# Adding the diagonal mask of turned attention scores on VectorE, in the banks, instead of with a product on TensorE

## The reference, cut to what matters

```python
s = einsum('bcgrd,bkgd->bcgrk', qc, keys) * 64 ** -0.5      # scores of a query with every key
p = masked_softmax(s, key_position <= query_position)       # exp(s - row maximum), other entries are zero
o = einsum('bcgrk,bkgd->bcgrd', p, values)
```

## Time and profile before

| what | value |
|---|---|
| time, median of 3 runs (range) | 895.42 us (895.35 to 897.48) |
| time of the profiled execution | 894.6 us |
| its span in the trace | 892.6 us |
| TensorE busy | 867.4 us (97% of the span) |
| VectorE busy | 611.5 us (69%) |
| ScalarE busy | 495.1 us (55%) |
| GpSimd busy | 174.0 us (19%) |
| nsa attention in the trace | from 145.3 us to about 211.8 us |
| moba attention in the trace | from 295.8 us to about 322 us |

### The profile page before, as it was taken

How to read it: one execution, slowest core, us unless ns; L and a number is a source line. 1 busy time by engine, 2 the same in 40 slices (tenths; PEclk the granted TensorE clock), 3 DMA queues, 4 the chain that set the end, 5 groups by cost and what they waited for, 6 DMA issues and landing times.

```text
span 892.6 us, 14774 instructions
## 1 busy us (share of the span) xinstructions
PE 867.4 (97%) x5801; PEld 789.1 (88%) x5801; DVE 611.5 (69%) x974; ACT 495.1 (55%) x782; POOL 174.0 (19%) x189
## 2 busy tenths in 40 slices
PE   3999999999999999999999999999999999999998
PEld 3789898998688989999998888799998999999886
DVE  5884788978868787666665556596668666666552
ACT  3634767564747656544444447687765644444431
POOL 1026355563054710000000004280000000000000
PEclk9999999999999999999999999999999999999999
DMA  9956655456472565666667555553345566665650
GB/s 362 364 204 212 213 189 190 124 177 208 138 258 88 189 209 160 198 189 189 189 189 216 160 155 186 165 165 95 115 124 175 178 194 188 186 188 186 205 176 24
DMA packets 45844, 163.38 MB, mean 183 GB/s; under 512 B 5200, under 2 KB 5584, under 8 KB 45776
## 3 DMA queue, kind: packets, MB, share of 16 engines
q1 hardware_dynamic: 45776, 162.44, 57.3%
HBM read 161.37 MB, written 1.05 MB: 182 GB/s over the span
## 4 chain that ended last, share of the span: by engine, by line
PE 87%; DVE 5%; ACT 4%; issue 2%; DMA 1%; SPq 0%; POOL 0%; DVEq 0%; ACTq 0%
PE bank L518 36%; PE bank L506 33%; PE bank L533 3%; PE bank L865 2%; PE bank L703 2%; PE bank L680 2%; DVE ada_acc L1748 1%; DMA x<-in_x 1%; PE bank L705 1%; PE bank L656 1%; PE bank L613 1%; PE bank L684 1%; ACT w_hi L1104 1%; DVE w_lo L1663 1%; PE bank L707 1%
## 5 line engine op out<-in xcount | busy, mean ns | idle before, releaser
L1104 ACT ACTIVATE w_hi<-w_raw 128x1024 fp32r<-128x1024 f32 (+2 forms) x249 | 259.5, 1049 | 224.7 <-PE bank L518 121.3
L1663 DVE TENSOR_TENSOR w_lo<-w_raw,w_hi 128x1024 fp32r<-128x1024 f32 (+2 forms) x249 | 301.4, 1221 | 76.4 <-ACT w_hi L1104 75.7
L518 PE MATMUL bank<-h_hi,w_hi 128*128 128x256 f32 x904 | 254.4, 281 | 0.2 <-ACT tok_k L1108 0.2
L518 PE MATMUL bank<-h_lo,w_hi 128*128 128x256 f32 x904 | 251.6, 278 | 0.0
L518 PE MATMUL bank<-h_hi,w_lo 128*128 128x256 f32 x904 | 251.5, 278 | 0.0
L518 PEld LDWEIGHTS bank<-h_lo,w_hi 128*128 128x128 f32 x904 | 171.3, 189 | 0.5 <-issue 0.2
L518 PEld LDWEIGHTS bank<-h_hi,w_hi 128*128 128x128 f32 x904 | 169.8, 188 | 1.3 <-issue 0.9
L518 PEld LDWEIGHTS bank<-h_hi,w_lo 128*128 128x128 f32 x904 | 169.7, 188 | 0.0
L506 PE MATMUL bank<-w_hi,h_hi 128*128 128x512 f32 (+1 forms) x240 | 95.7, 399 | 0.8 <-issue 0.5
L2533 POOL TENSOR_TENSOR ada_acc<-ada_acc,w_raw 128x512 f32<-128x512 f32 x56 | 82.3, 1471 | 68.4 <-ACT w_raw L1108 63.3
L506 PE MATMUL bank<-w_lo,h_hi 128*128 128x512 f32 (+1 forms) x240 | 93.1, 388 | 0.0
(11 more groups left out here) (321 smaller groups left out, 1402.8 us busy)
## 6 DMA issues: line engine op xcount, KB each, us to landing
w_raw<-in_weights SPq DMA_DIRECT2D x298, 512.0 KB, 4.3
w_raw<-in_weights SPq DMA_DIRECT2D x4, 360.0 KB, 3.5
x<-in_x SPq DMA_DIRECT2D x1, 1024.0 KB, 9.2
gate_row<-in_gate_bias SPq DMA_DIRECT2D x2, 512.0 KB, 7.0
out<-x SPq DMA_DIRECT2D x4, 256.0 KB, 3.2
w_raw<-in_weights SPq DMA_DIRECT2D x3, 256.0 KB, 2.7
const<-in_constants SPq DMA_DIRECT2D x1, 285.5 KB, 5.2
cols<-in_columns SPq DMA_DIRECT2D x1, 208.5 KB, 2.3
```

The lines of the kernel that those rows point to most:

```text
L518: mm = e.matmul(o, ws[p], xs[q], start=(k + kk == 0 and i == 0 and b % 2 == 0), stop=(k + kk == kts - 1 and i == 2 and (b % 2 == 1 or b == ...
L1104: e.activation(w_hi[i % NSPLIT][:, 0:c], raw[v % NRAW][:, 0:c], ACT.Copy).then_inc(*rounded(v))
L1663: e.tensor_tensor(w_lo[i % NSPLIT][:, 0:c], raw[v % NRAW][:, 0:c], w_hi[i % NSPLIT][:, 0:c].bitcast(F32), ALU.subtract).then_inc(*rested(v))
```

## The change

The mask product of each piece is gone from TensorE. A 128x128 matrix `keep` (0 where the key counts, -1e30 where not) is made once by VectorE, out of a constant, shortly before the nsa attention. After each piece's last product VectorE adds `keep` to the diagonal block of both heads, in place in the bank (128x256 elements), and the exponential waits for this addition (`kept`) and no longer for the product. In VectorE's loop the additions of (i, x=0) stand first in slot i, ahead of `evict(i-1)`, and those of (i, x=1) between `evict(i-1)` and the shifts of slot i+1. The mask products of the first pass (lines 654 and 659) stay.

```diff
@@ constants and signals
+        keep = sb("keep", [P, P], on=mix)
+        kept, keep_made = signal("kept"), signal("keep_made")
@@ turned_scores, TensorE
-                    e.matmul(o[:, :, 0:P], mask_r[:, :], bcast(unit_r[:, :].unsqueeze(1), [P, 2, P]), start=False,
-                             stop=False, skip_group_check=True)
@@ pair_attention, ScalarE
-                        w.wait_ge(*scored.at((s, i, x, 0)))
+                        w.wait_ge(*kept.at((s, i, x, 0)))
...
-                        w.wait_ge(*scored.at((s, i, x, 1)))
+                        w.wait_ge(*kept.at((s, i, x, 1)))
@@ pair_attention, VectorE
+                def keeps(i, x_):
+
+                    allowed = bcast(keep[:, :].unsqueeze(1), [P, 2, P])
+                    for j, o in enumerate(turned_items(x_)):
+                        diagonal = o[:, :, 0:P]
+                        w.wait_ge(*scored.at((s, i, x_, j)))
+                        e.tensor_tensor(diagonal, diagonal, allowed, ALU.add).then_inc(*kept((s, i, x_, j)))
...
                 for i in range(n + 3):
                     pr = slots[s][i - 2]["close"] if 0 <= i - 2 < n else None
+                    if i < n:
+                        keeps(i, 0)
                     if 0 < i <= n:
                         evict(i - 1)
+                    if i < n:
+                        keeps(i, 1)
                     for x_ in range(2 if i + 1 < n else 0):
                         shift(i + 1, x_)
@@ before the nsa attention, VectorE
+                    w.wait_ge(*const_in.at())
+                    e.tensor_scalar(keep[:, :], con("upto"), -NEG, NEG, ALU.mult, ALU.add).then_inc(*keep_made())
+                    w.wait_ge(*keep_made.at())
```

## The result

The changed kernel takes 912.28 us (median of 4 runs, 911.8 to 913.36) against 895.67 us of the kernel before on the same chip: 1.0188 times as long, with a 95% interval of 1.0176 to 1.02. That is 16.6 us slower, where +7.7 us was forecast, and above the range. The profiled execution took 912.71 us, with a span of 910.7.

What follows compares the result with a forecast made beforehand. TensorE, busy for 97% of the span, was taken to bound the kernel. nsa +3.7 and moba +4.0 gave +7.7 us: 902.3 against the profiled 894.6, a forecast median of 903.1 us, 8-in-10 range 898.7 to 908.5.

Steps and rivals of the forecast that it cites:

- The sign and the mechanism: Whole kernel: slower, chance 0.92; exponentials wait for VectorE's additions, 0.42 us each, standing behind other work, and TensorE waits.
- The clock falls: Rival: after moba slot 3's wait of some 4 us the clock drops to 1.2 GHz, 3 us more, 906.1; chance 0.12.
- nsa's layout: Eight nsa slots laid out engine by engine: TensorE's lateness ends at 3.7 us, the 3.8 us shed already taken off.
- The lateness comes to 0.7 us at slot 2: nsa: TensorE late at a slot's first scores by 0.7 us at slot 2, 1.2 at 3, 1.9 at 4, 3.4 at 5.
- The full round: nsa, around slot 4: VectorE's round of 8.15 us, only 0.7 idle, grows to 9.5 with four additions.
- the later slots cover most of the new chain: nsa after slot 5: TensorE's 2 us of other products per slot cover most of it; lateness goes from 3.4 to 3.7.
- Moba, +4.0: moba attention: two new waits, at slots 2 and 3, make it 4.0 us longer.
- the dear wait: moba slot 3: additions of (3, x=0) stand behind two low parts; TensorE idles some 4 us before (3, x=1)'s second piece.
- TensorE sheds 5.8 us: Both attentions: 48 mask products removed at 0.12 us each, 3.8 us in nsa and 1.9 in moba.
- The rival in which that time is simply gained: Rival: VectorE reaches each addition once scores are there, so the kernel takes 889.6 us; chance 0.05.

Runs made afterwards that it cites:

- the filler kernel: The changed kernel with 43 idle products of 512 columns put before score pieces at which TensorE had waited: 907.38 us, ratio 1.014.
- with the filler: Additions in nsa's slots 0 to 2 alone, products elsewhere, plus twelve overwritten products before slot 1's second scores: 901.71 us, against 903.11 without these twelve.
- The two loads: Kernel before plus 48 VectorE instructions of 128x256 that nobody waits for: additions with two SBUF inputs 925.83 us, multiplications with one 918.74 us.
- the one-move kernel: The changed kernel with additions of (i, x=0) ahead of low parts (nsa slots 4, 6, moba 3) and of the gate's column (moba 2): 910.28 us.

## Why the prediction failed

**The sign and the mechanism held.** The additions take 424 ns and are not stretched, and the waits lie on the chain addition, exponential, second piece. After moba nothing but the offset changed (17.5 us late at the turning and at the end, the 0.62 us taken off both). TensorE's idle time grew by 11.1 us (6.5 in the window of nsa, 4.5 in that of moba), against 13.5 foretold (7.5 and 6). In nsa that is near by luck: 3.2 us of its waits lie where none was foretold, and slow products fill others.

**"The clock falls" was a rival instead of a term.** This is about half of the 8.9 us that were missing. In the trace of the filler kernel, with a clock of 0.998, TensorE is 7.6 us late at the end of nsa and 4.9 more in moba, where 3.7 and 4.0 were foretold; the changed kernel, with its lower clock, has 5.0 more. So in these traces nsa's layout was short by 3.9 us, moba's by 0.9 and the clock by 5.0. The prediction itself had the sum of waits and a single one of some 4 us, and gave the clock a chance of 0.12 and a price of 3 us, as if it could fall once. It fell in both stages, stayed low for up to 10.2 us, and took 11.8 us from TensorE. The Trainium skill (TensorE: Matmul & The Clock Gate, What's actually happening), which the prediction cited as making this case likely, pointed the right way: a clock of 0.50 begins with the end of the wait of 3.23 us. The trace before, which had no wait in the middle of the work, was no evidence against it.

**"The lateness comes to 0.7 us at slot 2": it was 4.6, and 3.0 with the fillers.** My layout of nsa gave slot 0's hook to VectorE about 2 us too early and at the speed of before, so it saw no wait before (1, x=1). The trace has 3.23 us there. Slots 0 to 2 alone make 7.1 us in their trace, 4.1 at full clock with the filler, where 1.2 at slot 3 was foretold. That the two tiny instructions were stretched by GpSimd is read from the timelines, and no run tests it. Checking the layout against two starts of the kernel before, both later in nsa, could not find this: before, nobody waited for that hook.

**"The full round" at slots 3 and 4** was right. In the trace with these slots alone TensorE is 1.7 us late at slot 5 and 2.0 at moba's slot 0; the layout had 3.4 - 1.2 = 2.2. That the later slots cover most of the new chain was right too: 1.7 us alone and 0.9 inside the change, where 0.3 was foretold.

**Moba, +4.0.** The places and the 3.55 us of the dear wait were right. The stage alone cost 7.0; in the window behind the wait, at 0.58, the clock took (1 - 0.58) x 4.00 = 1.7 us from TensorE. Moving the additions ahead of the low parts took 3.3 us back (7.0 to 3.7), so the cause of this half is shown. What makes the other 3.7 was not taken apart.

**"TensorE sheds 5.8 us"** is true of its work and not of the time: 1.1 us, not clear of nothing, is what leaving out products and additions altogether gave. The rival in which that time is simply gained, 889.6, was out of reach: the kernel without any addition took 894.1.

**Open** stays how the nsa loss at full clock divides between VectorE's added work and the exponentials' wait. The two loads were meant to tell and didn't.

## What to carry to other kernels

An engine that is idle for 20% of a stage is no free engine if its list has hooks in it: look up what stands in front of each new instruction, and who begins to wait for work that nobody waited for before. When the forecast itself contains waits of 2 to 4 us on TensorE at full clock, put the lower clock into the sum: here it fell behind waits of 3.23, 3.55 and 1.96 us. And before counting removed work as gain, ask what the next chain is; leaving the work out altogether is a cheap run that tells it. And when parts of a change are measured by themselves, look in the trace whether the time was lost where the part is.

## What was unexpected in the hardware

- **The low clock does not follow the length of the wait alone.** The same wait of 1.98 us before the second piece of (4, x=1) was followed by 17 us at 0.52 on the mean in the kernel with additions in all of nsa, and by a clock of 1.00 in the one with slots 3 and 4 alone. Wait and sequel of each, as windows:

```profile
182.00:185.00 3.00, 1.02 (x5) 0.55 (x5) 2.93 (x9) 1.60 (x4) 2.71 (x3) 1.00 0.24 34
185.00:202.00 17.00, 17.00 (x69) 15.66 (x68) 8.58 (x23) 6.21 (x11) 5.98 (x5) 0.52 0.47 150
```

```profile
180.00:182.50 2.50, 0.52 (x3) 0.17 (x2) 2.43 (x8) 1.24 (x3) 2.33 (x2) 1.00 0.26 31
182.50:200.00 17.50, 17.17 (x125) 15.82 (x126) 12.63 (x28) 10.25 (x20) 9.38 (x7) 1.00 0.53 162
```

  In the first, TensorE was busy without a gap for 17 us and still ran near half the clock; that run was the slowest of its four (909.82 us). The scatter of such kernels goes with the clock: the one-move kernel took 906.99 us at a mean clock of 0.998 and 912.92 at 0.989, the kernel with slots 5 to 7 took 896.27 at 1.000 and 902.55 at 0.992.
- **Additions in a bank were not stretched beside GpSimd.** With one input in a bank they took 417 to 433 ns, though 14 of their 29 rows overlap a row of GpSimd; of the same shape with both inputs in SBUF, 407 to 1516; multiplications by a constant, with the one input in SBUF, 279 to 1376. The Trainium skill (SBUF — State Buffer, Who interferes with whom) names all three: two SBUF inputs contend with GpSimd's reads, a `tensor_scalar` can when it runs in a two-port mode, and one SBUF input outside these modes does not. The rows agree. So a stand-in for an instruction must have its operands in the same memories, or it measures something else.
